# First mixer of a two-block transformer kernel: the two maps' scores half a weight slot apart, retention scores by pairs of heads, two memory keys around the retention half's turn

## The reference

```python
def diff_attention(q, k, v, lam):          # 4 heads, 2 maps each, 64 wide
    ...
        s = jnp.einsum('bqhmd,bkhmd->bhmqk', qb, k).astype(jnp.float32) * scale
        p = jax.nn.softmax(s, axis=-1)
        a = p[:, :, 0] - lam * p[:, :, 1]
        return jnp.einsum('bhqk,bkhe->bqhe', a.astype(v.dtype), v)
...
def retention_direction(q, k, v, log_gamma, strict):   # 4 heads, 64 wide keys, 128 wide values
    ...
        inner = jnp.einsum('bhid,bhjd->bhij', qi, ki) * decay_in[None]
...
def first_block(...):
        h = rmsnorm(x, attn_norm_g[l])
        proj = h @ w_in[l]                                   # 1024 x 3072
        ...
        a = diff_attention(dq, dk, dv, lam)
        ...
        r = group_norm(r_fwd + r_bwd, ret_norm_g[l]).reshape(B, S, RET_WIDTH)
        r = jax.nn.silu(rg.astype(jnp.float32)) * r
        mix = jnp.concatenate([a, r], axis=-1).astype(x.dtype)
        x = x + mix @ w_out[l]
        x = x + peer_ffn(rmsnorm(x, ffn_norm_g[l]), ...)
...
def memory_attention(h, mem_h, wq, wk, wv, wo):
    k = (mem_h @ wk).reshape(b, -1, MEM_HEADS, MEM_HEAD_DIM)
```

## Time and profile before

| | |
|---|---|
| median of 3 runs | 1538.87 us (1535.15 to 1539.41) |
| span of the profiled execution | 1535.2 us; its own time is 1535.15 us or within a rounding of it |
| PE busy | 1487.8 us, 97% |
| PEld busy | 1343.8 us, 88% |
| DVE, ACT, POOL busy | 850.1 (55%), 760.9 (50%), 958.7 (62%) us |
| TensorE clock | full but for one stretch in the mixer, and the last microseconds |

### The profile page before, as it was taken

The page is one execution under the profiler, slowest core; times in us unless marked ns, Lnnn a source line. Parts: engine busy times, 40 slices in busy tenths (PEclk is TensorE's granted clock), DMA queues, the critical chain, the costliest instruction groups (busy, mean ns, idle before and its releaser), DMA issues.

```text
span 1535.2 us, 26609 instructions
## 1 busy us (share of the span) xinstructions
PE 1487.8 (97%) x9614; PEld 1343.8 (88%) x9614; DVE 850.1 (55%) x2084; ACT 760.9 (50%) x1270; POOL 958.7 (62%) x409
## 2 busy tenths in 40 slices
PE   7999999999999999999999999998899999999997
PEld 6677998999999888889999999987799789899996
DVE  4555289989998655532222222235477834366565
ACT  6456545454444544444444444456566456544444
POOL 6546888874455000048888888877754366588885
PEclk9999999999999999999999999999999999999999
DMA  7434656653334666655565655665533344366553
GB/s 245 134 110 135 178 182 231 188 180 104 115 120 118 187 196 195 196 173 186 190 183 186 191 183 186 190 205 179 178 110 97 127 128 144 116 186 182 187 183 118
DMA packets 69489, 254.17 MB, mean 166 GB/s; under 512 B 7776, under 2 KB 8032, under 8 KB 68768
## 3 DMA queue, kind: packets, MB, share of 16 engines
q1 hardware_dynamic: 67248, 244.35, 51.3%
q10 hardware_dynamic: 1728, 6.68, 1.2%
q0 software_dynamic: 432, 2.07, 0.4%
HBM read 249.91 MB, written 3.15 MB: 165 GB/s over the span
## 4 chain that ended last, share of the span: by engine, by line
PE 60%; issue 20%; POOL 16%; DVE 2%; ACT 1%; DMA 1%; POOLq 0%; ACTq 0%; DVEq 0%
PE bank L487 19%; PE bank L488 19%; PE bank L489 19%; POOL w_lo L452 15%; PE bank L878 4%; DMA ring<-weights_in 1%; POOL w_lo L446 0%; POOLq L462 0%; ACT w_hi L1367 0%; ACT h_hi L1436 0%; DVE xres L2073 0%; POOLq L451 0%; DVE work L2426 0%; DVE w_lo L2457 0%; DVE act_lo L2462 0%
## 5 line engine op out<-in xcount | busy, mean ns | idle before, releaser
L452 POOL TENSOR_TENSOR w_lo<-ring,w_hi 128x1024 fp32r<-128x1024 f32 x392 | 940.8, 2403 | 550.8 <-ACT w_hi L1367 544.3
L1367 ACT CAST w_hi<-ring 128x1024 fp32r<-128x1024 f32 x452 | 474.0, 1050 | 618.8 <-PE bank L489 588.8
L487 PE MATMUL bank<-h_hi,w_hi 128*128 128x256 f32 x1696 | 487.6, 288 | 3.7 <-POOL w_lo L452 2.8
L489 PE MATMUL bank<-h_hi,w_lo 128*128 128x256 f32 x1696 | 479.7, 283 | 0.0
L488 PE MATMUL bank<-h_lo,w_hi 128*128 128x256 f32 x1696 | 479.6, 283 | 0.0
L487 PEld LDWEIGHTS bank<-h_hi,w_hi 128*128 128x128 f32 x1696 | 324.6, 191 | 8.4 <-POOL w_lo L452 3.6
L488 PEld LDWEIGHTS bank<-h_lo,w_hi 128*128 128x128 f32 x1696 | 324.8, 192 | 3.5
L489 PEld LDWEIGHTS bank<-h_hi,w_lo 128*128 128x128 f32 x1696 | 324.4, 191 | 0.0
L487 PE MATMUL bank<-w_hi,act_hi 128*128 128x512 f32 x600 | 234.9, 391 | 4.4 <-DVE act_lo L2462 1.5
L488 PE MATMUL bank<-w_lo,act_hi 128*128 128x512 f32 x600 | 234.5, 391 | 0.0
L489 PE MATMUL bank<-w_hi,act_lo 128*128 128x512 f32 x600 | 233.4, 389 | 0.0
(11 more groups left out here) (410 smaller groups left out, 1851.0 us busy)
## 6 DMA issues: line engine op xcount, KB each, us to landing
ring<-weights_in SPq DMA_DIRECT2D x463, 512.0 KB, 3.5
mem_kv<-arena ACTq DMA_DIRECT2D x2, 1024.0 KB, 6.9
arena<-mem_kv ACTq DMA_DIRECT2D x2, 1024.0 KB, 6.8
xres<-x_in SPq DMA_DIRECT2D x2, 512.0 KB, 6.6
arena<-mem_in POOLq DMA_DIRECT2D x1, 1024.0 KB, 8.8
arena<-rows_in ACTq DMA_DIRECT2D x2, 512.0 KB, 4.9
arena<-consts_in POOLq DMA_DIRECT2D x1, 512.0 KB, 10.7
arena<-consts_in ACTq DMA_DIRECT2D x2, 256.0 KB, 5.6
```

The lines of the kernel that those rows point to most:

```text
L452: nc.gpsimd.tensor_tensor(w_lo[:, k, :], ring[:, k, :], w_hi[:, k, :].bitcast(F32), ALU.subtract)\
L487: pe.matmul(out_, a[0], b[0], start=start, stop=False, **kw)
L489: return pe.matmul(out_, a[1], b[0], start=False, stop=stop, **kw)
L1367: nc.scalar.copy(w_hi[:, k, :], ring[:, k, :]).then_inc(s["hi_made"], 1)
```

## The change

Three parts. First, `diff_scores` is called for one map at a time: map 0 of unit u + 1 where both stood, map 1 after the half slot that followed, just ahead of `diff_turn(u)`. Second, `ret_scores` is called twice, each time for a pair of heads, with the two heads' matmuls in turn (array rows 0 to 63 to bank 4, rows 64 to 127 to bank 5); the second pair stands after `ret_out(1)`, where head 3's scores stood. Third, memory keys 1 and 2 move ahead of the last four `w_out` slots: key 1 before the wait for the retention half and its turn, key 2 behind the turn. The order of slots, the casts in ACT's list and ACT's copies of the two keys follow. No instruction's shape changes and none is added or removed but these moves.

```diff
@@ _steps @@
-            stage(name, range(SLOT[name], SLOT[name] + n))
+            stage("w_out", range(SLOT[name], SLOT[name] + 4))
+            stage("mem_k_second", [SLOT["mem_k"] + 1, SLOT["mem_k"] + 2])
+            stage("w_out_late", range(SLOT[name] + 4, SLOT[name] + n))
@@ tensor @@
-            def diff_scores(u):
+            def diff_scores(u, m):
                 h, t = units[u]
-                if u >= 2:
+                r = slice(m * 64, m * 64 + 64)
+                if m == 1:
+                    pe.wait_ge(s["diff_scores"], 2 * u + 1)
+                elif u >= 2:
                     pe.wait_ge(s["diff_mixed"], u - 1)
...
             for u in range(len(units)):
                 if u + 1 < len(units):
-                    diff_scores(u + 1)
+                    diff_scores(u + 1, 0)
                 in_unit(26 + 2 * u)
+                if u + 1 < len(units):
+                    diff_scores(u + 1, 1)
                 diff_turn(u)
                 in_unit(27 + 2 * u)
                 diff_out(u)
...
-            def ret_scores(h):
-                r = slice((h % 2) * 64, (h % 2) * 64 + 64)
-                if h >= 2:
-                    pe.wait_ge(s["ret_decayed"], h - 1)
+            def ret_scores(pair):
+                if pair:
+                    pe.wait_ge(s["ret_decayed"], 2 * pair)
                 for j in range(TT):
-                    mm = pe.matmul(bank[:, 4 + h % 2, j * T:(j + 1) * T], ...)
-                mm.then_inc(s["ret_scores"], 1)
+                    for e in range(2):
+                        r = slice(e * 64, e * 64 + 64)
+                        mm = pe.matmul(bank[:, 4 + e, j * T:(j + 1) * T], ...)
+                        if j == 1:
+                            mm.then_inc(s["ret_scores"], 1)
...
             for k in range(4):
                 out_slot(k, "mix_d")
+            mem_key(1)
             pe.wait_ge(s["head_mixed"], 3)
             half_turn("mix_r", lambda b, t: mix[:, t, 512 + b * P:512 + (b + 1) * P], 6)
+            mem_key(2)
             for k in range(4, KD):
                 out_slot(k, "mix_r")
             low("mix_r", 3)
-            for j in range(1, 8):
+            for j in range(3, 8):
                 mem_key(j)
@@ scalar @@
-            hi_parts(28 + NS)
+            hi_parts(KEY_SLOT[1] + NS)
+            mem_k_copied(1)
             turned_hi("mix_r", h_t, 4, lambda b: stat[:, 97 + b:98 + b], bank0=6, first=4)
+            hi_parts(KEY_SLOT[2] + NS)
             nc.scalar.activation(warm_1[:, :], ident[:, 0:1], ACT.Sqrt)
-            hi_parts(STEP["w_out"] + KD - 1 + NS)
+            hi_parts(OUT_SLOT[4] + NS)
+            mem_k_copied(2)
+            hi_parts(OUT_SLOT[7] + NS)
```

More of the change, by code:

```diff
@@ L105, in _steps @@
             stage("mem_k_first", [SLOT["mem_k"]])
-            stage(name, range(SLOT[name], SLOT[name] + n))
+            stage("w_out", range(SLOT[name], SLOT[name] + 4))
+            stage("mem_k_second", [SLOT["mem_k"] + 1, SLOT["mem_k"] + 2])
+            stage("w_out_late", range(SLOT[name] + 4, SLOT[name] + n))
         elif name == "mem_k":
-            stage(name, range(SLOT[name] + 1, SLOT[name] + n))
+            stage(name, range(SLOT[name] + 3, SLOT[name] + n))
         elif name == "xbc":
@@ L190 @@
 QUERY_SLOT = [STEP["queries"] + i for i in range(19)] + [STEP["last_keys"]]
-KEY_SLOT = [STEP["mem_k_first"]] + [STEP["mem_k"] + i for i in range(7)]
+KEY_SLOT = [STEP["mem_k_first"]] + [STEP["mem_k_second"] + i for i in range(2)] + [STEP["mem_k"] + i for i in range(5)]
+OUT_SLOT = [STEP["w_out"] + i for i in range(4)] + [STEP["w_out_late"] + i for i in range(4)]
 VALUE_SLOT = [STEP["mem_v_first"] + i for i in range(2)] + [STEP["mem_v"] + i for i in range(6)]
@@ L666, in _ @@
             units = [(h, t) for h in range(HD) for t in range(TT)]
-            def diff_scores(u):
+            def diff_scores(u, m):
                 h, t = units[u]
-                if u >= 2:
+                r = slice(m * 64, m * 64 + 64)
+                if m == 1:
+                    pe.wait_ge(s["diff_scores"], 2 * u + 1)
+                elif u >= 2:
                     pe.wait_ge(s["diff_mixed"], u - 1)
[L672 to L678, removed]
+                pe.matmul(bank[:, 4 + u % 2, m * T:(m + 1) * T], qk_t[r, h, t * P:(t + 1) * P],
+                          qk_t[r, 4 + h, :], start=True, stop=True).then_inc(s["diff_scores"], 1)
             def diff_turn(u):
@@ L698, in _ @@
             pe.wait_ge(s["turned_out_dve"], TURN["qk"][2] + 2)
-            diff_scores(0)
+            diff_scores(0, 0)
+            diff_scores(0, 1)
             in_unit(25)
@@ L715, in half_turn @@
                     mm.then_inc(s["turned"], 1)
-            def ret_scores(h):
-                r = slice((h % 2) * 64, (h % 2) * 64 + 64)
-                if h >= 2:
-                    pe.wait_ge(s["ret_decayed"], h - 1)
+            def ret_scores(pair):
+                if pair:
+                    pe.wait_ge(s["ret_decayed"], 2 * pair)
                 for j in range(TT):
-                    mm = pe.matmul(bank[:, 4 + h % 2, j * T:(j + 1) * T], qk_t[r, 10 + h // 2, j * P:(j + 1) * P],
-                                   qk_t[r, 8 + h // 2, :], start=True, stop=True)
-                mm.then_inc(s["ret_scores"], 1)
+                    for e in range(2):
+                        r = slice(e * 64, e * 64 + 64)
+                        mm = pe.matmul(bank[:, 4 + e, j * T:(j + 1) * T], qk_t[r, 10 + pair, j * P:(j + 1) * P],
+                                       qk_t[r, 8 + pair, :], start=True, stop=True)
+                        if j == 1:
+                            mm.then_inc(s["ret_scores"], 1)
             def ret_out(h):
@@ L744, in _ @@
             in_unit(43)
-            ret_scores(1)
             pe.wait_ge(s["diff_out_copied"], 8)
@@ L749, in _ @@
                 ret_out(h)
-                if h + 2 < HD:
-                    ret_scores(h + 2)
                 if h == 1:
+                    ret_scores(1)
                     low("mem_a", 3)
@@ L756, in out_slot @@
             def out_slot(k, ready):
-                n = STEP["w_out"] + k
+                n = OUT_SLOT[k]
                 wait_slot(pe, n)
@@ L1588, in _ @@
                 act.wait_ge(s["norm_summed"], 2 * NORMS["ffn"] + t + 1)
-                hi_parts(KEY_SLOT[1] + NS + t)
+                hi_parts(KEY_SLOT[3] + NS + t)
             act.wait_ge(s["norm_mean"], NORMS["ffn"] + 1)
             nc.scalar.activation(rstd[:, 0:2], ssq[:, 2:4], ACT.Sqrt).then_inc(s["norm_rooted"], 1)
-            mem_k_copied(1)
+            mem_k_copied(3)
             act.wait_ge(s["norm_factor"], NORMS["ffn"] + 1)
             nc.scalar.mul(x_scaled[:, 0, :], xres[:, 0, :], rstd[:, 2:3]).then_inc(s["norm_scaled"], 1)
-            for j in range(2, 6):
+            for j in range(4, 6):
                 hi_parts(KEY_SLOT[j] + 1 + NS)
@@ L2312, in _ @@
                     else:
-                        dve.wait_ge(s["spent"], STEP["w_out"] + KD)
+                        dve.wait_ge(s["spent"], OUT_SLOT[7] + 1)
                     v.tensor_tensor(xres[:, t, h * 512:(h + 1) * 512], xres[:, t, h * 512:(h + 1) * 512],
```

## The result

| | before | after |
|---|---|---|
| median | 1538.87 us (1533.82 to 1540.65, 7 runs) | 1541.94 us (1538.86 to 1545.65, 7 runs) |
| ratio to before | | 1.0033, 95% interval 1.0018 to 1.0047 |
| span of the profiled execution | 1535.2 us | 1537.0 us (its time 1538.86) |
| PE, ACT busy | 1487.8, 760.9 us | 1485.6, 760.7 us |

The change makes the kernel slower by 0.33%, 5.1 us by the ratio (2.8 to 7.2). The two medians lie 3.1 us apart, which is inside that interval too. The forecast was +5.0 us.

The account below looks back on a forecast made before the run. It took the differential units to be bound by the chain of scores, DVE, ACT's copy and output (5.34 us), not PE's work. +9.9 - 1.5 - 3.4 = +5.0 on the 1538.87 median gave 1543.9 us, range 1536.5 to 1549.

Parts of the forecast that it names:

- Part 1, +9.9: Differential units: later map 1 scores delay ACT's copy and the output, unit 5.34 to 6.81 us; +9.9 us in all.
- Rival 1: Differential units: the delay is hidden before ACT's copy and the change pays; -6.4 us, 1532.5; chance 0.10.
- Part 2, -1.5: Retention scores by pairs of heads: matmuls on different array rows overlap in part, gaining 1.5 us.
- rival 2: Retention scores: pairs run side by side in full, 1.06 us each, gain 2.2; total +4.3, 1543.2; chance 0.18.
- Part 3, -3.4: Keys 1 and 2 around the retention half's turn: gain 3.4 us, some 1.8 waiting and 1.6 slow clock.
- The sum: Whole kernel: +9.9 - 1.5 - 3.4 = +5.0 us, 1543.9 against the median.
- Rivals 3 and 4: Clock falls in differential units, 1546 up to 1564; or retention pairs cost or clock falls elsewhere, 1546; together 0.12.
- rival 4: Retention pairs cost, or the clock falls outside the units and takes back 1.6: +7, 1546; within a shared 0.12.
- The FFN norm: After the slots: three keys (8.6 us), not five, cover DVE's norm, 7.24 us; it still fits by 1.4.

Follow-up runs that it names:

- parts 2 and 3: Kernel after with part 1 undone, both maps' scores together again: ratio 0.9968 (0.9955 to 0.9982), 4.9 us faster than before.
- part 1 alone: Kernel before with only the two maps' scores set half a slot apart: ratio 1.0073 (1.0060 to 1.0087), 11.2 us slower.

## Why the prediction was right, point by point

**Part 1, +9.9.** Measured +9.8. The step from map 0's start to DVE's maximum was put at 2.95 and is 2.94; the unit at 6.81 and is 6.79. PE's wait was put at some 1.7 and is 1.5. That the copy is what carries the delay was argued from handovers within 0.05 us; moving the cast shortened the unit by just the cast, and moving the copy ended the wait. Rival 1 is refuted.

**Part 2, -1.5.** Mis-sized: 2.5. The forecast allowed overlap only in part, because a float32 matmul shows as two records; the pair shows full overlap, which was rival 2's price of 2.2. The other 0.3 are changes between 128-row matmuls and the scores: the sum counted one of them, 0.08, but they go at both single scores that are dropped. The two half slots around head 1's scores took 3.08 us and take 2.87, head 0's output took 0.99 and takes 0.81.

**Part 3, -3.4.** Right for the pair of traces (3.5), but mis-sized for what the runs compare. The sum took the slow clock of 134.4 as a cost of the waits that comes each time. It came in one of six traces. Its mean worth is then 1.9 + 1.6 / 6 = 2.2, an estimate from six traces.

**The sum.** +9.8 - 2.5 - 2.2 = +5.1, the ratio's own value, though its interval of 2.8 to 7.2 could not tell this from 4 or 6. The mechanism of part 1, which sets the sign, was right. That the forecast's +5.0 was so close was luck: two errors of 1.0 and 1.2 us cancelled. Rival 2's mechanism was true without its result, and a part of part 3's gain was an accident of one execution. The parts alone fit the same values within their intervals: +11.2 (9.2 to 13.4) for part 1, where 9.8 was due, and -4.9 (-6.9 to -2.8) for parts 2 and 3, where -4.7 was.

**Rivals 3 and 4.** The clock did not stay low in the units with PE waiting over a fifth of the time; it fell there once, in one of the three traces with these waits. The pairs of rival 4 cost nothing. Its other half, a fall elsewhere that takes back 1.6, is what the two profiled executions show: one fall each before the last microseconds, at 134 us before and at 1197 after.

**The FFN norm** behind three keys was not waited for: key 5's last matmul is followed by the norm's turn without a gap, as forecast.

**Open.** The spans of the two profiled executions differ by 1.8 and not 3.8 us, although the clock's fall at 1197 us adds 1.6 to the later one. Matmul by matmul the kernel after is 3.6 us behind at 170 us, 3.7 at 1043 and 0.3 at 1112: some 3.4 us come back in the second block, which the change does not touch. There PE's waits differ between traces of the same kernel too (one of 2.4 us for ACT in the first trace of before, one of 3.7 without a named cause in the second). What sets them was not tried. In the same way part 1 alone is 9.5 us behind at 1043 and 12.9 at the end, and the kernel before differs from itself: its second trace is 1.7 us ahead of the first at 1043 and 0.8 at 1131. So a few us of difference between the spans of two traces can come from there. That parts 2 and 3 each gain alone was shown by traces; by the runs alone each is below what they can tell.

## What to carry to other kernels

When a producer's instruction is moved later, follow each consumer's own list: what stands behind the waiting instruction on that engine moves with it, though it needs nothing of what was moved. Here ACT's copy of one unit stood behind the exponentials of the next, and reordering ACT was worth more than all that PE's list could give. And before a loss by a slow clock is booked as a cost of the waits ahead of it, look at more traces of the same kernel.

## What was not expected of the hardware

Two pairs of 64-row float32 matmuls on different halves of the array ran fully side by side in both orders, 1.06 to 1.08 us for four against 1.06 for two. A POOL subtraction (2.4 us alone, 2.9 in the first case) held up the DVE products beside it: two took 3.48 us and not 1.28, and where it ran beside the third instead, that one took 2.58 and not 0.69. And after the same waits the granted clock fell (0.61 over 4.4 us) in one trace of six.
